# Attention fillers one slot ahead, narrow gate projections as the loaded operand, a position table spread during the values, and scan loads ahead of a wait

## The chip, the cores and the metric

One core of a Trainium2 chip runs the whole program in one launch. The metric is the device time of the execution in microseconds; the kernel before took 3352.78 us, the median of three runs (3352.01 to 3353.17). All arithmetic is float32.

## The reference, cut to what matters

The program is two stacks of layers over 256 tokens of width 2048, one behind the other. The parts that the change touches:

```python
# first block, second layer: attention with three branches and a gate for each of 16 heads x 3
q, g, z = split(h @ w_qg)            # g: 48 columns, z: 3 x 2048 columns
out = sum over branches b of sigmoid(g_b) * attend_b(q, k_b, v_b) * silu(z_b)
x = x + gate * (out @ w_o)           # then the final rmsnorm
# second block: proj = u @ w_in, 11 parts, among them q, k, v and z of a gated delta rule,
q, k, v, beta_logit, a_logit = ...   # beta_logit, a_logit: 8 columns each
for each of 8 heads:                 # chunks of 64 tokens
    T = solve(I + L)                 # triangular, L from k k^T, decay and beta
    scan over 4 chunks with state S
# block attention with a bias by relative distance: rel_bias[bucket(distance), head]
s = q k^T * scale + rel_bias[bucket(i - j), h]
mix = sigmoid(gate_a) * (y_a @ w_gdn) + sigmoid(gate_b) * (y_b @ w_moba)
h = h + mix @ w_out                  # then a gated feed-forward of width 5632
```

## The kernel before, in words

Activations lie transposed: a tensor of 2048 features by 256 tokens is 16 tiles of 128 partitions by 256 columns (`hT`, `xT`). Weights come from HBM in slots of 2 MB, 256 output columns each, through a ring of three (`late_raw`) once the first stages are over; SP issues the loads in program order, and the load of slot n waits until TensorE has finished slot n-3 (`late_load`). Every engine works through one list of instructions in the order written.

A plain slot (`late_plain`) is 32 matmuls, weights as the loaded operand and the activations (256 columns) as the moving one. A split slot (`late_split`, stages in `SPLIT`) saves an eighth of them by sums that VectorE makes of the weights (`dve_sums`, `dve_last_sum`) and of the activations (`dve_half_sums`, once a stage): seven blocks of eight steps, of which the third waits for `late_sums`, the sixth for `late_last`. VectorE joins the parts (`dve_join`). A plain slot is copied out of PSUM by ScalarE (`late_drain`).

Order of the stages on TensorE that matter here: q, gates, zc (8 split slots), attention with the 16 plain slots of zs as fillers, o (output projection), gdn (12 slots), za, qb, kb, vb (4 each), the scan with ga as filler, gb, the second attention with gb2 as filler, the mix (bra, brb), out2, the feed-forward.

The attention works four head groups g, each in six units u (three branches by two token halves: `UNITS`). A unit is: scores on TensorE, mask and maximum on VectorE, exponential on ScalarE, sums and weights on VectorE (`p_ready`), transposes on TensorE, a copy to SBUF by ScalarE (`pT_kept`), values on TensorE (`o_ready`), and VectorE's product with the gate tile `zn` (`o_used`). Between these TensorE runs fillers, counted in matmuls: `FILL0` ahead of a group, and for each unit a number ahead of its transposes and one behind them. In group g they are the zs slots 4g to 4g+3, which hold the gate tiles of the same group; VectorE waits for their drains in units 2 and 4 (`wait_out` in `dve_attend`).

The gates (48 columns) and beta (16 columns) are computed with the activations as the loaded operand: 32 matmuls of 128 tokens each, with 48 or 16 moving columns (`pe_gates`, `pe_beta`).

The delta rule's triangular system is solved on VectorE (`dve_solve`) while TensorE does za, qb, kb, vb. SP moves the system in (`sp_solve`, through `scratch_L`) and the solution out and in again (`sp_solved`, through `scratch_T`), which stands in SP's list between the loads of vb and of ga. ScalarE stages each head of the scan (`act_scan`), then TensorE transposes it.

The position bias: a one-hot table by distance times `rel_bias` (`pe_bias`) gives a row for each head, which goes to HBM (`scratch_R`) and comes back with shifted rows (`sp_bias`). All of it stands behind the first gb slot and the sums of the norms; the mask is added in `dve_qkb`, behind VectorE's norms.

## Time and profile before

| | us or share |
|---|---|
| median of three runs | 3352.78 |
| profiled execution: its own time, span | 3352.57, 3350.8 |
| TensorE busy, weight loads, VectorE, ScalarE | 95%, 87%, 51%, 14% |
| chain that ended last | TensorE 78%, DMA 9%, VectorE 9%, issue 2% |
| attention, its four windows (1137 to 1466) | TensorE busy 303.29 of 329.00, granted clock 0.95 to 0.96 |
| one head group, from scores to scores | 82.2 |
| one split slot (112 records) in the chain of waits | 12.6 |
| a load of 2 MB, issue to landing, median | 8.4 |
| ScalarE's drains of the third and the last vb slot start | 1979.98, 1993.80 |
| granted clock, mean | 0.975 |

How to read it: a row of the timeline is a run of like instructions, with its start and length; the bracket tells how long the engine was idle before, and what ended that. A float32 matmul shows as two records, so x64 are 32 matmuls. The granted clock is a share of 2.4 GHz. Idle time of an engine off the chain costs nothing. TensorE's records overlap a little, so the distance of two starts tells more than a length.

### The profile page before, as it was taken

Reading aid. Unit: us, or ns where it says so; the run is one execution under the profiler, and the core shown is the slowest. Engines: PE = TensorE matmul, PEld = TensorE weight load, DVE = VectorE, ACT = ScalarE, POOL = GpSimd, SP = SyncE. Lnnn points to the kernel's source line nnn. Section 1 sums busy time; section 2 is a strip of 40 time slices with the busy share of each in tenths; the row PEclk is TensorE's granted clock in tenths of the full one; section 3 lists DMA queues with packets and bytes.
Section 4 is the critical chain, followed back from the end, with each engine's and each line's share of the span. In section 5 each row is a group of like instructions: output and inputs, shape, how many; then the busy total and the mean of one; then the engine's idle time right before and its main releaser. Section 6 shows DMA issues by size and latency. Waiting matters only on the chain.

```text
span 3350.8 us, 54055 instructions
## 1 busy us (share of the span) xinstructions
PE 3195.2 (95%) x22956; PEld 2905.7 (87%) x22956; DVE 1721.0 (51%) x2637; ACT 453.2 (14%) x798; POOL 138.0 (4%) x89
## 2 busy tenths in 40 slices
PE   6999998979999999989999999989999999999999
PEld 3777787868889977779888888879999999999999
DVE  5357634453244333346364765566665655555443
ACT  2114410000000122211220002211000000000000
POOL 0003310100000000002000000000010000000000
PEclk8999999989999999999999999999999999999999
DMA  9763457657473322224234442242544444444443
GB/s 409 313 276 127 188 236 320 262 213 289 175 298 150 141 109 107 101 104 173 101 137 179 153 160 101 101 146 97 182 177 154 173 175 157 169 175 157 169 163 138
DMA packets 50952, 599.37 MB, mean 179 GB/s; under 512 B 9511, under 2 KB 12086, under 8 KB 13278
## 3 DMA queue, kind: packets, MB, share of 16 engines
q1 hardware_dynamic: 50782, 596.88, 46.1%
q8 instruction: 134, 2.20, 0.3%
q14 instruction: 36, 0.29, 0.0%
HBM read 593.70 MB, written 3.16 MB: 178 GB/s over the span
## 4 chain that ended last, share of the span: by engine, by line
PE 78%; DMA 9%; DVE 9%; DVEq 2%; issue 2%; SPq 1%; ACT 1%; POOLq 0%; POOL 0%; ACTq 0%
PE bank L2496 24%; PE bank L771 16%; PE bank L720 13%; PE bank L286 9%; DMA ring<-in_t_mod 6%; PE bank L316 3%; DVE E L356 3%; DVE W L2008 2%; PE bank L328 2%; DVE W L2010 1%; PE bank L394 1%; PE aux L1593 1%; PE bank L546 1%; PE aux L1550 1%; PE bank L536 1%
## 5 line engine op out<-in xcount | busy, mean ns | idle before, releaser
L720 PE MATMUL bank<-hT,ring 128*128 128x256 f32 x2496 | 558.4, 383 | 4.3 <-DMA ring<-in_t_ga 4.3
L720 PEld LDWEIGHTS bank<-hT,ring 128*128 128x128 f32 x2496 | 475.9, 192 | 84.6 <-issue 16.8
L2496 PE MATMUL bank<-arena,ring 128*128 128x128 f32 x3440 | 396.4, 275 | 0.0
L2496 PEld LDWEIGHTS bank<-arena,ring 128*128 128x128 f32 x3440 | 390.2, 192 | 0.0
L286 PE MATMUL bank<-arena,ring 128*128 128x256 f32 x1536 | 342.5, 386 | 29.3 <-DMA ring<-in_t_kv 8.9
L286 PEld LDWEIGHTS bank<-arena,ring 128*128 128x128 f32 x1536 | 295.9, 194 | 72.2 <-issue 14.6
L771 PE MATMUL bank<-hT,ring 128*128 128x128 f32 x2624 | 323.0, 278 | 0.0
L771 PEld LDWEIGHTS bank<-hT,ring 128*128 128x128 f32 x2624 | 308.6, 194 | 6.0 <-issue 5.6
L286 PE MATMUL bank<-hT,ring 128*128 128x256 f32 x1024 | 228.0, 385 | 9.2 <-DVE hT L978 4.8
L286 PEld LDWEIGHTS bank<-hT,ring 128*128 128x128 f32 x1024 | 196.8, 193 | 37.8 <-DMA ring<-in_t_q 5.0
L2496 PE MATMUL bank<-hT,ring 128*128 128x128 f32 x1680 | 197.9, 275 | 0.0
L2496 PEld LDWEIGHTS bank<-hT,ring 128*128 128x128 f32 x1680 | 192.7, 192 | 0.1
L356 DVE SCALAR_TENSOR_TENSOR E<-ring,c_act,E 128x512 f32<-128x512 f32 x240 | 182.8, 762 | 18.5 <-issue 0.7
L771 PE MATMUL bank<-arena,ring 128*128 128x128 f32 x1472 | 175.5, 275 | 0.0
L771 PEld LDWEIGHTS bank<-arena,ring 128*128 128x128 f32 x1472 | 170.2, 192 | 0.3
L2587 DVE TENSOR_TENSOR arena<-bank,w_gate 128x256 f32<-128x256 f32 x50 | 21.2, 424 | 204.0 <-ACT rstd L2535 132.5
L2496 PE MATMUL bank<-arena,E 128*128 128x128 f32 x1024 | 119.7, 275 | 0.0
L2496 PEld LDWEIGHTS bank<-arena,E 128*128 128x128 f32 x1024 | 117.0, 192 | 0.0
L316 PE MATMUL bank<-hT,ring 128*128 128x256 f32 x512 | 116.8, 387 | 0.0
L316 PEld LDWEIGHTS bank<-hT,ring 128*128 128x128 f32 x512 | 97.4, 193 | 15.1 <-issue 0.4
L2008 DVE TENSOR_TENSOR W<-E,arena 128x128 f32<-128x128 f32 (+7 forms) x64 | 74.8, 1168 | 44.7 <-issue 27.8
L354 DVE TENSOR_SCALAR E<-ring,c_act 128x512 f32<-128x512 f32 x16 | 8.5, 532 | 168.1 <-DMA ring<-in_t_mod 166.1
(425 smaller groups left out, 3692.2 us busy)
## 6 DMA issues: line engine op xcount, KB each, us to landing
ring<-in_t_mod SPq DMA_DIRECT2D x64, 2048.0 KB, 13.7
ring<-in_t_gu SPq DMA_DIRECT2D x44, 2048.0 KB, 8.2
ring<-in_t_out SPq DMA_DIRECT2D x16, 2048.0 KB, 8.4
ring<-in_t_zs SPq DMA_DIRECT2D x16, 2048.0 KB, 8.4
ring<-in_t_down SPq DMA_DIRECT2D x16, 2048.0 KB, 7.4
ring<-in_t_gdn SPq DMA_DIRECT2D x12, 2048.0 KB, 8.4
ring<-in_t_u SPq DMA_DIRECT2D x8, 2048.0 KB, 8.9
ring<-in_t_z SPq DMA_DIRECT2D x8, 2048.0 KB, 8.6
```

The lines of the kernel that those rows point to most:

```text
L286: last = nc.tensor.matmul(bank[s][:, T * f:T * f + T], w[:, j, P * f:P * f + P], act[:, j, :], start=j == 0, stop=j == kd - 1)
L316: last = nc.tensor.matmul(bank[s][:, T * f:T * f + T], w[:, j, P * f:P * f + P], act[:, j, :], start=j == 0, stop=j == KD - 1)
L328: last = nc.tensor.matmul(bank[s][:, T * f:T * f + T], act[:, j, P * f:P * f + P], w[:, j, :], start=j == 0, stop=j == KD - 1)
L356: nc.vector.scalar_tensor_tensor(a, w, c_act[:, j:j + 1], a, ALU.mult, ALU.add)
L394: last = nc.tensor.matmul(out[32 * q:32 * q + 32, :], c_act[:, j:j + 1].to_broadcast([P, 32]), w[:, j, :], start=a == 0, stop=a == KD // 4 ...
L536: last = nc.tensor.matmul(out[:, T * f:T * f + T], w[:, j, P * f:P * f + P], x[:, j, :], start=j == 0 and f == 0, stop=j == KD - 1 and f == 1)
L546: last = nc.tensor.matmul(out[:, T * f:T * f + T], w[:, j, P * f:P * f + P], x[:, j, :], start=j == 0, stop=j == KD - 1)
L720: last = nc.tensor.matmul(out[:, T * f:T * f + T], w[:, j, P * f:P * f + P], act[:, j, :], start=j == 0, stop=j == kd - 1)
L771: last = nc.tensor.matmul(out[:, P * at:P * at + P], a[:, j, :], tile_at(b, j), start=j == 0 and q in (0, 3), stop=j == half - 1 and q in ...
L1550: last = nc.tensor.matmul(aux[:, nk * h:nk * h + nk], qg[:, h, P * f:P * f + P], keys, start=True, stop=True)
L2008: v.tensor_tensor(tmp, Tsol[:, :, 0:J], row, ALU.mult)
L2496: last = nc.tensor.matmul(out[:, P * q:P * q + P], a[:, j, :], b[:, j, :], start=begins and q == 0 and j == 0, stop=ends and q == len(grou ...
```

## The change

```diff
+def pe_o_first(pe, act, first, count):
+    n = LBASE["o"]
+    w = late_raw[n % LRING][:].rearrange("p (j n) -> p j n", n=SLOT_COLS)
+    out = late_bank(n)[0]
+    old = KD - HPG
+    order = [(f, j) for heads in (range(old), range(old, KD)) for f in range(2) for j in heads]
+    if first == 0:
+        late_ready(pe, n)
+        pe.wait_ge(att_ready, KV - 1)
+    for m in range(first, first + count):
+        f, j = order[m]
+        if m == 2 * old:
+            pe.wait_ge(att_ready, KV)
+        last = nc.tensor.matmul(out[:, T * f:T * f + T], w[:, j, P * f:P * f + P], act[:, j, :],
+                                start=m == 0, stop=m == 2 * KD - 1)
+    if first + count == 2 * KD:
+        last.then_inc(late_done, 1)
...
             late_split(pe, name, s, quarters(act), t_all, (at, at))
+        elif name == "o":
+            pe_o_first(pe, act, O_AHEAD, 2 * KD - O_AHEAD)
...
 gates_ready = sem("gates_ready")
...
+gate_fold, gate_rows = W[:, 1920:1984], W[:, 1664:1920]
+beta_fold, beta_rows = W[:, 1536:1568], W[:, 1280:1536]
...
+    for j in range(KD // 2):
+        for q in range(4):
+            k, first = j + KD // 2 * (q // 2), 16 * (q % 2)
+            last = nc.tensor.matmul(A(3, T, T)[32 * q:32 * q + 32, :], w_gate[:, k, first:first + 32], hT[:, k, :],
+                                    start=j == 0, stop=j == KD // 2 - 1)
+    last.then_inc(gates_summed, 1)
+def pe_gates_fold(pe):
+    pe.wait_ge(folds_ready, 1)
+    pe.wait_ge(gates_raw, 1)
     for f in range(TT):
-        for j in range(KD):
-            last = nc.tensor.matmul(A(3, 48 * f, 48), hT[:, j, P * f:P * f + P], w_gate[:, j, :],
-                                    start=j == 0, stop=j == KD - 1)
+        for at, first, n in ((0, 0, 16), (16, 32, 32)):
+            last = nc.tensor.matmul(A(3, 48 * f + at, n), gate_rows[:, P * f:P * f + P], gate_fold[:, first:first + n],
+                                    start=True, stop=True)
...
+def act_gates_raw(act):
+    act.wait_ge(gates_summed, 1)
+    nc.scalar.copy(gate_rows, A(3, T, T)).then_inc(gates_raw, 1)
...
     for s in range(LCOUNT["zc"]):
+        if s == 1:
+            act_gates(act)
...
 def dve_zc(dve):
+    nc.vector.tensor_tensor(gate_fold, ident[:, 0:64], ident[:, 64:128], ALU.add).then_inc(folds_ready, 1)
...
-FILL0, FILL = 10, [(12, 4), (12, 4), (18, 4), (22, 4), (16, 4), (18, 0)]
-ENDS = {}
-_done = FILL0
-for _u, _pieces in enumerate(FILL):
-    for _place, _count in enumerate(_pieces):
-        for _slot in range(_done // (2 * KD), (_done + _count) // (2 * KD)):
-            ENDS[_slot] = (_u, _place)
-        _done += _count
+FILL0 = 10
+FILLS = [[(12, 4), (12, 4), (18, 4), (22, 4), (14, 4), (18, 2)]] * (KV - 1)
+FILLS += [[(10, 4), (10, 4), (12, 4), (18, 4), (16, 4), (0, 0)]]
+O_FILL = (20, 4)
+O_AHEAD = sum(O_FILL)
+ENDS = []
+for _fill in FILLS:
+    _done, _ends = FILL0, {}
+    for _u, _pieces in enumerate(_fill):
+        for _place, _count in enumerate(_pieces):
+            for _slot in range(_done // (2 * KD), (_done + _count) // (2 * KD)):
+                _ends[_slot] = (_u, _place)
+            _done += _count
+    ENDS.append(_ends)
 def act_attend(act):
+    def gate_slot(s):
+        at = 4 * (s // 4) + HEADS * (1 + s % 4 // 2) + 2 * (s % 2)
+        late_drain(act, "zs", s, zn[:, at:at + 2, :], ACT.Silu)
...
         for k in range(4):
-            if ENDS[k] == (u, place):
-                at = 4 * g + HEADS * (1 + k // 2) + 2 * (k % 2)
-                late_drain(act, "zs", 4 * g + k, zn[:, at:at + 2, :], ACT.Silu)
+            if 4 * g + k + 1 < LCOUNT["zs"] and ENDS[g][k] == (u, place):
+                gate_slot(4 * g + k + 1)
+    gate_slot(0)
...
     pe.wait_ge(kc_kept, 1)
+    late_plain(pe, "zs", 0, hT)
     for g in range(KV):
+        FILL = FILLS[g]
...
                 n = min(count, 2 * KD - first)
-                late_plain(pe, "zs", 4 * g + k, hT, first, n)
+                late_plain(pe, "zs", 4 * g + k + 1, hT, first, n)
...
             done += FILL[u][0]
+            if (g, u) == (KV - 1, ATT - 1):
+                pe_o_first(pe, tiles(B(1)), 0, O_FILL[0])
...
             done += FILL[u][1]
+            if (g, u) == (KV - 1, ATT - 1):
+                pe_o_first(pe, tiles(B(1)), O_FILL[0], O_FILL[1])
...
             v.tensor_tensor(z, z, zn[:, ds(4 * g + HEADS * br, 4), :], ALU.add)
-    dve.drain().then_inc(att_ready, 1)
+        dve.drain().then_inc(att_ready, 1)
...
+def dve_fold_beta(dve):
+    v = nc.vector
+    v.tensor_tensor(beta_fold[:, 0:16], ident[:, 0:16], ident[:, 32:48], ALU.add)
+    v.tensor_tensor(beta_fold[:, 16:32], ident[:, 64:80], ident[:, 112:128], ALU.add)
+    dve.drain()
+    v.tensor_tensor(beta_fold[:, 0:16], beta_fold[:, 0:16], beta_fold[:, 16:32], ALU.add).then_inc(folds_ready, 1)
...
+    flat = w_beta[:].rearrange("p j n -> p (j n)")
+    for j in range(KD // 4):
+        for q in range(4):
+            k = 4 * j + q
+            first = 16 * k - (16 if q == 3 else 0)
+            last = nc.tensor.matmul(A(3, T, T)[32 * q:32 * q + 32, :], flat[:, first:first + 32], hT[:, k, :],
+                                    start=j == 0, stop=j == KD // 4 - 1)
+    last.then_inc(lg_summed, 1)
+def pe_beta_fold(pe):
+    pe.wait_ge(folds_ready, 2)
+    pe.wait_ge(lg_raw, 1)
     for f in range(TT):
-        for j in range(KD):
-            last = nc.tensor.matmul(A(3, 16 * f, 16), hT[:, j, P * f:P * f + P], w_beta[:, j, :],
-                                    start=j == 0, stop=j == KD - 1)
+        last = nc.tensor.matmul(A(3, 16 * f, 16), beta_rows[:, P * f:P * f + P], beta_fold[:, 0:16],
+                                start=True, stop=True)
...
+def act_beta_raw(act):
+    act.wait_ge(lg_summed, 1)
+    nc.scalar.copy(beta_rows, A(3, T, T)).then_inc(lg_raw, 1)
...
     pe.wait_ge(norm_inv, 1 if part == 0 else 2)
-    pe.wait_ge(rel_kept, 1)
...
         dve_sums(dve, "gb", s + 2)
+        if s == 1:
+            dve_bias(dve)
...
 flip, causal_flip = B(2, 3072, P), B(2, 3072 + P, P)
-onehot = B(4, 0, 512)[0:32]
-rel = B(4, 512, 8)[0:32]
-by_dist = B(4, 1024, 512)[0:GH]
+onehot = [st[0][0:32], st[4][0:32]]
+rel = W[0:32, 2000:2008]
+by_dist = [st[6][0:GH], W[0:GH, 1744:2000]]
...
+def sp_rel(sp):
+    sp.wait_ge(head_done, GH + 1)
+    for k in range(2):
+        sp.dma_start(onehot[k], t["onehot"][:, T * k:T * k + T]).then_inc(rel_in, 16)
+    sp.dma_start(rel, t["rel_bias"]).then_inc(rel_in, 16)
+def sp_rel_out(sp):
+    sp.wait_ge(rel_kept, 1)
+    for k in range(2):
+        sp.dma_start(t["scratch_R"][:, T * k:T * k + T], by_dist[k]).then_inc(rel_out, 16)
...
-    sp.wait_ge(oh_kept, GH + 1)
-    sp.dma_start(onehot, t["onehot"]).then_inc(rel_in, 16)
-    sp.dma_start(rel, t["rel_bias"]).then_inc(rel_in, 16)
-    sp.wait_ge(rel_kept, 1)
-    sp.dma_start(t["scratch_R"], by_dist).then_inc(rel_out, 16)
-    sp.wait_ge(rel_out, 16)
+    sp.wait_ge(rel_out, 32)
...
 def pe_bias(pe):
-    pe.wait_ge(rel_in, 32)
-    nc.tensor.matmul(A(3)[0:GH], rel, onehot, start=True, stop=True).then_inc(rel_ready, 1)
+    pe.wait_ge(rel_in, 48)
+    pe.wait_ge(head_done, GH)
+    for k in range(2):
+        last = nc.tensor.matmul(A(3, T * k, T)[0:GH], rel, onehot[k], start=True, stop=True)
+    last.then_inc(rel_ready, 1)
...
     act.wait_ge(rel_ready, 1)
-    nc.scalar.copy(by_dist, A(3)[0:GH]).then_inc(rel_kept, 1)
+    nc.scalar.copy(by_dist[0], A(3, 0, T)[0:GH])
+    nc.scalar.copy(by_dist[1], A(3, T, T)[0:GH]).then_inc(rel_kept, 1)
...
     for s in range(LCOUNT["vb"]):
+        if s == 3:
+            act_bias(act)
...
-def dve_qkb(dve):
+def dve_bias(dve):
...
+def dve_qkb(dve):
...
     sp_solve(sp)
-    for name in ("qb", "kb", "vb"):
+    for name in ("qb", "kb"):
         late_stream(sp, name)
+    sp_rel(sp)
+    late_stream(sp, "vb")
+    late_stream(sp, "ga", 0, 2)
     sp_solved(sp)
-    for name in ("ga", "gb"):
-        late_stream(sp, name)
+    sp_rel_out(sp)
+    late_stream(sp, "ga", 2)
+    late_stream(sp, "gb", 0, 3)
     sp_bias(sp)
+    late_stream(sp, "gb", 3)
...
         late_split(pe, "zc", s, h_quarters, zc_halves, (ZC_H, ZC_H))
+        if s == 0:
+            pe_gates_fold(pe)
     pe_attend(pe)
-    pe.wait_ge(att_ready, 1)
...
         else:
-            late_plain(pe, "gdn", s, hT, ready=(h_ready, 12) if s == AHEAD else None)
+            late_plain(pe, "gdn", s, hT)
+        if s == AHEAD - 1:
+            pe.wait_ge(h_ready, 16)
+            pe_beta(pe)
         if s == AHEAD:
-            pe_beta(pe)
+            pe_beta_fold(pe)
...
         for s in range(LCOUNT[name]):
+            if name == "vb" and s == 3:
+                pe_bias(pe)
             late_plain(pe, name, s, hT, rows=name == "vb")
+    pe.wait_ge(rel_kept, 1)
...
             pe_norm_sums(pe)
-            pe_bias(pe)
...
     drain_to(act, "q", q_all, ACT.Copy, SCALE)
-    act_gates(act)
+    act_gates_raw(act)
...
         act_raw(act, s)
+        if s == AHEAD - 1:
+            act_beta_raw(act)
...
     act_norms(act)
-    act_bias(act)
...
     dve_final0(dve)
+    dve_fold_beta(dve)
```

In words: the zs slot 0 is computed and drained ahead of the first group, and each filler is a matmul of the slot after the one it was; the last group fills with the rest of zs and with 24 of the 32 matmuls of o's slot 0, first those of the heads whose groups are done (`pe_o_first`). The gates and beta load 32 weight columns at a time and move 256 columns of activations, four column groups of the array side by side, each summing its share of the 16 tiles; ScalarE copies the four partial sums, and a matmul with stacked identities (`gate_fold`, `beta_fold`) adds and transposes them. The table product runs ahead of the last vb slot from other buffers, in two halves; its rows go out behind the solver's exchange and come back behind the norms' sums, ahead of the last gb load. The mask is added in VectorE's norms. The first two ga loads stand ahead of SP's wait for the solver.

## Rows read from the trace of the kernel before

**Rows 1.** The waits of TensorE, whole span: us in total, times, longest.

```profile
PE aux L1582 <- DVE arena L1631: 17.9, 4, 4.7
PE aux L2324 <- DVEq L2299: 4.6, 1, 4.6
```

**Rows 2.** Timeline, attention's first group: start, length, engine, line, tile, count, [idle, releaser].

```profile
1169.96 9.66 PE L720 MATMUL bank<-hT,ring 128*128 128x256 f32 x44
...
1174.30 1.23 DVE L1631 TENSOR_TENSOR arena<-arena,small 128x1024 f32<-128x1024 f32 x1
...
1204.98 0.69 DVE L1650 TENSOR_TENSOR arena<-arena,aux 128x512 f32<-128x512 f32 x1 [7.22 <-ACT arena L790]
...
1208.64 1.82 PE L1582 MATMUL aux<-con,arena 128*128 128x128 f32 x8 [4.38 <-DVE arena L1631]
1211.57 3.78 PE L1593 MATMUL aux<-arena,W 128*128 128x512 f32 x4 [1.10 <-ACT arena L1536]
...
1219.72 0.96 PE L1550 MATMUL aux<-W,arena 128*128 128x15 f32 x8
```

**Rows 3.** Windows, TensorE, same group: stretch, us, busy, granted clock, DMA share, GB/s.

```profile
1211.00:1216.00 5.00, 4.43 (x7) 0.53 0.02 7
```

**Rows 4.** Timeline, end of the attention.

```profile
1465.17 15.58 PE L720 MATMUL bank<-arena,ring 128*128 128x256 f32 x64 [3.42 <-DVEq L1656]
...
1467.73 2.52 DVE L861 TENSOR_TENSOR hT<-arena,hT 128x1024 f32<-128x1024 f32 x2
...
1472.87 1.22 DVE L818 TENSOR_TENSOR ring<-ring 128x1024 f32<-128x1024 f32 x1
```

**Rows 5.** Windows, then timeline, around the beta matmuls.

```profile
1616.00:1620.00 4.00, 4.00 (x20) 0.50 0.68 287
...
1611.95 10.87 PE L1765 MATMUL aux<-w_beta,hT 128*128 128x16 f32 x64
...
1622.66 17.02 PE L720 MATMUL bank<-hT,ring 128*128 128x256 f32 x64
```

**Rows 6.** Timeline, gates and the start of zc.

```profile
1022.72 9.12 PE L1470 MATMUL aux<-w_gate,hT 128*128 128x48 f32 x64
...
1025.58 2.52 DVE L861 TENSOR_TENSOR arena<-hT,arena 128x1024 f32<-128x1024 f32 x2
...
1031.64 5.29 PE L771 MATMUL bank<-hT,ring 128*128 128x128 f32 x32
```

**Rows 7.** Timeline, row products of the modulation, in four column groups.

```profile
61.93 3.61 PE L394 MATMUL bank<-ring,c_act 128*32 128x256 f32 x32 [2.42 <-DMA ring<-in_t_mod]
...
247.90 1.93 PE L394 MATMUL bank<-ring,c_act 128*32 128x256 f32 x32
249.76 0.42 PE L1228 MATMUL bank<-arena,E 32*32 32x128 f32 x8
```

**Rows 8.** Chain of waits, scratch_T's landings, then timeline, around the solver's end.

```profile
1787.69 10.28 DMA scratch_L<-E
...
1984.68 2.60 DMA scratch_T<-E
...
DMA to landing us min/median/max: 2.6/3.8/4.7
...
1996.31 0.38 ACT L2044 COPY W<-small 128x2 f32<-128x2 f32 x3
1998.04 6.29 PE L720 MATMUL bank<-hT,ring 128*128 128x256 f32 x14 [4.28 <-DMA ring<-in_t_ga]
```

**Rows 9.** Timeline, norms and position table behind the first gb slot.

```profile
2187.60 6.55 DVE L2220 RECIPROCAL W<-W 128x1024 f32<-128x1024 f32 x1
2188.68 1.87 PE L2279 MATMUL aux<-arena 32*8 32x512 f32 x2 [6.19 <-DMA arena<-in_rel_bias]
...
2196.63 1.22 DVE L825 TENSOR_TENSOR ring<-ring 128x1024 f32<-128x1024 f32 x1 [0.67 <-PE bank L771]
2205.46 1.14 PE L2209 MATMUL aux<-W,ones 1*128 1x512 f32 x8
```

More of the change, by code:

```diff
@@ L1395, in build @@
         gates_ready = sem("gates_ready")
+        gates_summed = sem("gates_summed")
+        gates_raw = sem("gates_raw")
+        folds_ready = sem("folds_ready")
+        gate_fold, gate_rows = W[:, 1920:1984], W[:, 1664:1920]
+        beta_fold, beta_rows = W[:, 1536:1568], W[:, 1280:1536]
         gates_kept = sem("gates_kept")
@@ L1689, in build @@
         qk_ready = sem("qk_ready")
+        lg_summed = sem("lg_summed")
+        lg_raw = sem("lg_raw")
         lg_ready = sem("lg_ready")
```

## The prediction

> **What bounds the kernel now.** I read the waits of TensorE first, since the page shows it busy 95% of the span and the chain of waits is 78% TensorE, then the timeline around each wait, then the granted clock around it. The reader is to see two things. The waits in the changed stretch are few but each costs twice: TensorE stands still, and when it resumes its records are twice as long for some microseconds. In the last unit of a head group, TensorE sits idle 4.38 us, for a softmax weight that VectorE wrote late, then 1.10 us for a copy [rows 2]; the granted clock right behind is 0.53 of 2.4 GHz, close to the 1.2 GHz level [rows 3]. There are four such waits, 17.9 us [rows 1]. Second, matmuls with few moving columns lower the clock without any idle time: after the 64 narrow records of the beta projection the clock is 0.50 [rows 5]. The triangular solver on VectorE fills part of the chain, but it runs beside TensorE's projections and starts when TensorE ends the first za slot (SP's loads wait for it), so it moves with TensorE.
>
> All times below are on the profiled execution (3352.57 us, span 3350.8), which lies 0.2 us under the median of the three runs. The rate at full clock: 44 records of a 256-column projection take 9.50 us from start to start of the next group, 0.216 us a record, and a matmul has two records, so 0.432 us [rows 2].
>
> **Fillers one slot ahead.** Why TensorE waits in unit 5: VectorE's product for unit 4 waited 7.22 us for the ScalarE drain of the fourth gate slot [rows 2], and that slot's matmuls are unit 5's own 18 fillers. Only behind it come the weights, done at 1208.59. One slot ahead, the drain lies in unit 4, and unit 5 should look like unit 3, which has the same shape: there the weights end at 1175.53, 5.6 us behind the start of the fillers (1169.96), while 18 fillers last 7.8 us [rows 2]. So 2.2 us of slack and no wait. Before, from the end of the fillers (1204.26, that is 1208.64 less 4.38) to the next scores at 1219.72 are 15.5 us. After: eight transposes 0.9 (half of 1.82), two fillers 0.86, and the copy still decides, which lets the values start 2.2 us behind the transposes (0.2 to its start, 1.0 for it); values 1.8 at full rate (half of 3.78, less the tail), ten fillers 4.3: 8.2 us. With the 0.86 us of fillers that unit 4 gives up, a group gains 8.1 us, three groups 24.4.
>
> The last group holds 96 gate fillers and 24 matmuls of the output projection's first slot; 116 of them come ahead of unit 5's transposes where 128 did: 5.2 us less; from there to the projection's start the 14.7 us become 7.8 (transposes, four fillers, values, then the same 3.42 us for VectorE's product and two additions [rows 4]), 6.9 more. In front stands the first gate slot, +13.8. So the attention's end comes 24.4 + 5.2 + 6.9 - 13.8 = 22.7 us earlier, and with 24 of the 32 matmuls done. The remaining eight want 3.5 us and about 1.8 more at half rate (the old 64 records took 15.58 instead of 13.8 [rows 4]). They end about when VectorE's half sums are there, 5.1 us behind the start (1470.25 against 1465.17 [rows 4]), and the next slot's first two blocks, 3.6 us, end at 8.9 us, when its weight sums end too (1474.09 [rows 4]). What was 15.4 us becomes 5.3: 10.1 more. **Sum 32.8 us.** I looked for what is late next. ScalarE now drains slot 0 before it stages the first group, beside ten fillers (4.3 us against some 2.9 of copies and drain): covered by 1.4 us. In the last group the drain of the last gate slot stands in front of the exponential of unit 5; 20 fillers (8.6 us) stand over a VectorE chain of about 6.2 us from the end of that unit's subtraction. If each group kept 1 us of wait the sum would be 29; if the half-rate stretch behind the attention went too, 34.5.
>
> **Narrow beta.** Removed: 64 records in 10.7 us, and the slot behind them at 16.9 instead of 13.8, since the clock was 0.50 [rows 5]. Added: 32 records in four column groups, a form the kernel has already: 32 records of a 32-column stationary in 1.93 us [rows 7], 1.86 to the next instruction; and a fold of four narrow records, 0.45. ScalarE's copy (about 0.5) and VectorE's three small additions (0.7) lie beside the slot between. 10.7 + 2.9 (the slot to the next instruction) - 1.86 - 0.45 = **11.3 us**. If the four groups did not overlap, 32 records at 0.216 would be 6.9 instead of 1.9, and 6.4 would be left; nothing else can gain more than 12.
>
> **Narrow gates.** Here the cover is the point. Removed: 64 records in 8.8 us, and 1.5 of the slowed start of the next slot (32 records in 5.29 [rows 6]; at 12.5 us for a split slot's 112 they are 3.6). Added: 64 records at the same form, 3.7 us, and a fold of eight, 0.9. But VectorE's half sums, which this long block hid, end at 1028.10 [rows 6], and the new small addition puts them to 1028.4. TensorE would be ready at 1026.3 and waits 2.1 us. An idle of 2.42 us was followed by 32 records of 3.61 instead of 1.93 us [rows 7], so I price a half-rate stretch at 2 us. Slot 0 began at 1031.5 and ended at 1045.6 (12.5 for a split slot, and the 1.5); now 1028.4 + 12.5 + 2 + 0.9 = 1043.8: **1.8 us**. The gates' sigmoid now stands between ScalarE's first and second zc copies; queued behind it is a copy that VectorE's join wants 5 us into slot 1, and the fold is done at its start, so it costs nothing. Without the clock's fall 3.8; with four groups not overlapping, a loss of 6.
>
> The Trainium skill, TensorEngine Tiling (Array Packing), Key Properties, says that changing the tiling mode drains TensorE; that speaks against both edits. Of the drain the rows show at most 0.2 us, the block of 32 records ending 1.86 us after its start [rows 7]. By that rule, with one matmul's latency of 0.38 us at each of the four changes, an estimate, the forecast would be 1.5 us later.
>
> **Scan loads ahead of the solver's wait.** The solver ends at 1984.68 and its result goes out (2.60 us) and back (up to 4.7) [rows 8], so it is back near 1992. But the scan's first weights are issued behind that: TensorE waits 4.28 us and its first 14 records then take 6.29 instead of 3.0 [rows 8], and the transposes come at 2004.3. ScalarE had staged the head by 1996.69 [rows 8]. Now two slots are loaded. The new cost is the queue: the second is issued when the third value slot ends (about 1979.8), still moving (8.4 us a slot on the page) when the solver's result goes out at 1984.7. The nearest row: the solver's input, issued right behind such a load, landed after 10.28 [rows 8]. From the load's end at 1988.4, half a megabyte takes about 2, so 1990.3, and back at 1995.0. TensorE ends the last value slot at 1994.4 (0.8 later, for the position matmuls, now four records), does the seven fillers to 1997.5, ScalarE stages 2.1 us from 1995.2: transposes at 1997.7. **6.5 us.** Bounds: 7.3 if the exchange isn't delayed, 2 if it waits the full 10.28. SP's issue of the second load is ready 5 us before the solver ends, so the wait does not move. The two new waits on SP, for the heads ahead of the table's loads (with vb's loads queued behind) and for the table's copy ahead of the third ga load, are met some 100 us and some 10 us before they are reached.
>
> **Position table.** Removed: 6.19 us of TensorE's wait, 1.87 for the matmul at half rate, and 2.4 of slow records in the slot behind, which lasts from 2190.55 to 2205.46 where 12.5 would do [rows 9]. But VectorE takes over: its two reciprocals end at 2194.15 [rows 9], whatever TensorE does, and the last-sum of the second gate slot follows a join of 1.8, so it ends near 2197.4 where it ended at 2197.85 [rows 9]. TensorE starts the slot at 2182.5, has five of its seven blocks by 2191.4, and stands for 6.0 us; the two last blocks (3.6 us) then run at half rate, 7.1, to 2204.6 against 2205.5: 0.9 gained out of 10. The other half of the edit is better: the wait of 4.6 us at the second attention [rows 1] ends, since VectorE adds the mask inside its norms, 2.5 us that are covered by a slot of 12.5; with the half-rate stretch behind it (1.5) that is 6.1. **7.0 us**, I take 7.2 with the small shifts. Bounds: 4 if that mask or its transfer (behind nothing now, ahead of one load) is late, 11 if the clock stays up in the stalled slot.
>
> **The sum.** 32.8 + 11.3 + 1.8 + 6.5 + 7.2 = 59.6; 3352.6 - 59.6 = 3293.0 for the execution profiled, and with the 0.2 of the median still **3293 us**. Up to the mix after the second attention nothing but TensorE's queue decides, so the terms add; the feed-forward part is unchanged.
>
> **Rivals.** (1) The solver's exchange is late, chance 0.13. SP has one queue, and the load of 2 MB in front is the change's own. The Trainium skill, DMA: Bandwidth & Descriptors, Queues, rings and completion order, says that descriptors of one ring are consumed in order, so the small transfer cannot overtake. With 10.28 us from 1984.7 it is back at 1999.7, TensorE idles 4.4 us, transposes at 2002: 4.3 us lost, and 2 at half rate: 3299. For it: the row of the solver's input. Against it: that one was issued 0.4 us behind its load, this one about 4.9. (2) Attention keeps a wait in unit 5, chance 0.12: ScalarE's table loads around the moved drains make the exponential late, 2 us a group, and the half rate returns with it (3 us): four times 5 is 20, 3313. For it: each drain between two exponentials brings ScalarE two more table loads. Against it: 2.2 us of slack in unit 3, which has the same chain. (3) The narrow forms do not overlap, 0.04: 5 + 8 lost, 3306. (4) Slower than before, 0.01: with its idle stretches gone, TensorE is granted less in the attention. That must cost over 60 us; the four groups have 303 us of busy TensorE at a mean of 0.96, so it decides below a mean of about 0.8. Against it: the unbroken stretches are at 1.00.
>
> **How the numbers follow.** The forecast has 0.70, its own range 3287 to 3300: the clock in the two stalled places is worth +5 and -2, the bounds of attention +4 and -2. To hold 8 in 10 I reach into rivals 1 and 2: 3286 to 3304. A difference under 0.2% (6.7 us) could not be told from no change. No case but the fourth comes near it: faster 0.98, same 0.01, slower 0.01.
>
> **What would show it.** In the waits, the line of the transposes (L1582) keeps no wait over 0.5 us; if it does, rival 2. A group takes 74 us instead of 82.2. The slot behind the beta matmuls lasts 13.8. The zc stage opens with an idle of 2.1 us behind VectorE's half sums; the second gb slot shows a new idle of about 6 us behind its last-sum, and the second attention none. The transposes of the scan follow the last value slot by about 3.3 us; more than 5 means rival 1. I am wrong in the main if the four attention groups together give less than 28 us.

## The result, and the profile after

The kernel after takes 3292.35 us, the median of four runs (3288.40 to 3293.69); the kernel before, timed beside it, 3352.40 (3350.68 to 3353.17). The ratio is 0.982, interval 0.9805 to 0.9834. The profiled execution took 3291.9 us with a span of 3289.8 and a granted clock of 0.984 (before 0.975). The forecast was 3293.

The changed stretches can be compared to 0.1 us, since each begins and ends with an instruction that both timelines have; the last one alone scatters between executions, by up to 1.7 us (see after_again). All lengths here are from start to start:

| from ... to | before | after | gained | forecast |
|---|---|---|---|---|
| start, first gate matmul | 1022.72 | 1024.54 | -1.8 | 0 |
| first gate matmul, slot 1 of zc | 22.98 | 19.61 | 3.4 | 1.8 |
| slot 1 of zc, slot 1 of o | 434.89 | 402.08 | 32.8 | 32.8 |
| slot 1 of o, the first of the two gdn slots at beta | 117.55 | 117.93 | -0.4 | 0 |
| from there, over both slots and beta, to the 32 records behind them (L1887, L1976 after) | 42.67 | 31.33 | 11.3 | 11.3 |
| these 32 records, the scan's transposes | 363.36 | 357.08 | 6.3 | 6.5 |
| the scan's transposes, the last row of TensorE | 1339.78 | 1330.38 | 9.4 | 7.2 |
| sum | | | 61.0 | 59.6 |

The first line is no part of the change: the stages ahead of the gates are the same code, and over all profiles of this document the first gate matmul starts between 1020.56 and 1025.41 us.

The first view is the waits of TensorE from 1000 to 2300 us, after (us in total, times, longest). To be seen: the 17.9 us of the transposes and the 4.6 of the second attention [rows 1] have no successor. Three waits over 1 us are new, behind VectorE's L847, L1533 and L606; the 3.4 us behind L1718 stood there before [rows 4].

```profile
PE bank L792 <- DVEq L847: 5.8, 1, 5.8
PE bank L524 <- DVEq L1718: 3.4, 1, 3.4
PE bank L792 <- DVEq L1533: 2.0, 1, 2.0
PE bank L792 <- DVEq L606: 1.5, 1, 1.5
...
PE aux L1655 <- ACT arena L1591: 0.7, 3, 0.2
```

The timeline of unit 5 in the first head group, after, answers to [rows 2]. VectorE's product for unit 4 (L1712) waits for nobody, the weights are done at 1213.37, and the fillers end 2.4 us behind them; only the copy leaves TensorE idle, for 0.24 us.

```profile
1207.80 7.93 PE L741 MATMUL bank<-hT,ring 128*128 128x256 f32 x36
...
1209.15 0.68 DVE L1712 TENSOR_TENSOR arena<-arena,aux 128x512 f32<-128x512 f32 x1
...
1212.14 1.23 DVE L1693 TENSOR_TENSOR arena<-arena,small 128x1024 f32<-128x1024 f32 x1
1215.57 1.04 PE L1642 MATMUL aux<-con,arena 128*128 128x128 f32 x8
...
1217.71 1.98 PE L1655 MATMUL aux<-arena,W 128*128 128x512 f32 x4 [0.24 <-ACT arena L1591]
```

The windows view of TensorE over one whole head group, after (us, busy, granted clock, DMA share, GB/s): busy 73.69 of 73.93 us at full clock, where [rows 3] showed 0.53 behind the wait.

```profile
1150.87:1224.80 73.93, 73.69 (x353) 1.00 0.32 122
```

The end of the attention answers to [rows 4]. After the 3.43 us for VectorE's last additions come the remaining eight matmuls of the output projection's first slot, then a wait of 1.53 us for its half sums.

```profile
1440.97 3.72 PE L524 MATMUL bank<-arena,ring 128*128 128x256 f32 x16 [3.43 <-DVEq L1718]
1446.23 3.81 PE L792 MATMUL bank<-arena,ring 128*128 128x128 f32 x32 [1.53 <-DVEq L606]
```

Beta after answers to [rows 5]: 1.86 us to the next start instead of 10.71, the slot behind it at full rate, and the fold of four records.

```profile
1564.16 1.93 PE L1841 MATMUL aux<-hT,w_beta 128*32 128x256 f32 x32
1566.02 14.08 PE L741 MATMUL bank<-hT,ring 128*128 128x256 f32 x64
1579.94 0.51 PE L1850 MATMUL aux<-W 128*128 128x16 f32 x4
```

The gates after answer to [rows 6]: 64 records in 3.66 us, a wait of 1.97 us for the half sums, records at full rate behind it, and a second wait of 0.32 us, for the first slot's weight sums.

```profile
1024.54 3.66 PE L1498 MATMUL aux<-hT,w_gate 128*32 128x256 f32 x64
1030.17 3.81 PE L792 MATMUL bank<-hT,ring 128*128 128x128 f32 x32 [1.97 <-DVEq L1533]
1034.30 5.62 PE L792 MATMUL bank<-arena,ring 128*128 128x128 f32 x48 [0.32 <-DVEq L840]
```

SP's queue after, around the solver's end, answers to [rows 8]: the solver's result goes out at 1939.97, and SP, which waits until it has landed, goes on at 1944.24, after 4.27 us.

```profile
1934.65 0.33 SPq L711 DMA_DIRECT2D ring<-in_t_ga  x1
1939.97 0.33 SPq L2082 DMA_DIRECT2D scratch_T<-E  x1
1944.24 1.35 SPq L2086 DMA_DIRECT2D E<-scratch_T  x2
```

And the stretch of the norms after, timeline, answers to [rows 9]: no table any more, but the second gb slot stands for 5.78 us until VectorE has done both reciprocals, a join and the last sum.

```profile
2132.59 3.35 DVE L2306 RECIPROCAL W<-W 128x512 f32<-128x512 f32 x1 [8.17 <-ACT W L2278]
2136.06 6.55 DVE L2308 RECIPROCAL W<-W 128x1024 f32<-128x1024 f32 x1
2144.55 1.22 DVE L846 TENSOR_TENSOR ring<-ring 128x1024 f32<-128x1024 f32 x1
2145.86 3.64 PE L792 MATMUL bank<-hT,ring 128*128 128x128 f32 x16 [5.78 <-DVEq L847]
2149.33 1.95 PE L792 MATMUL bank<-E,ring 128*128 128x128 f32 x16
```

### The profile page after: what moved, and what is told of

It is laid out like the page before. It is cut to its first block, busy times and chain, and to the rows that moved or that the text cites. A ratio compares the mean times of both kernels' runs of the same rounds, so it can differ in the third digit from the quotient of the medians.

```text
span 3289.8 us, 54033 instructions
## 1 busy us (share of the span) xinstructions
PE 3160.6 (96%) x22938; PEld 2877.1 (87%) x22938; DVE 1723.0 (52%) x2641; ACT 453.8 (14%) x801; POOL 139.8 (4%) x89
## 4 chain that ended last, share of the span: by engine, by line
PE 84%; DMA 8%; DVE 5%; DVEq 1%; issue 1%; ACT 0%; SPq 0%; POOLq 0%; POOL 0%; ACTq 0%
PE bank L2600 24%; PE bank L741 18%; PE bank L792 16%; PE bank L286 10%; DMA ring<-in_t_mod 7%; PE bank L316 3%; DVE E L356 3%; PE bank L738 2%; PE bank L328 2%; PE bank L394 1%; PE bank L567 1%; PE aux L1608 1%; PE bank L557 1%; PE aux L1655 1%; DMA ring<-in_t_kv 1%
## 5 line engine op out<-in xcount | busy, mean ns | idle before, releaser
L286 PEld LDWEIGHTS bank<-arena,ring 128*128 128x128 f32 x1536 | 296.8, 194 | 73.1 <-issue 14.7
```

Of the source, the lines that this page charges most:

```text
L286: last = nc.tensor.matmul(bank[s][:, T * f:T * f + T], w[:, j, P * f:P * f + P], act[:, j, :], start=j == 0, stop=j == kd - 1)
```

## The experiments

All were made from the kernel after. The times of one kernel scatter by some 3 us between executions, so each verdict rests on the length of its own stretch in one profile. no_o, long_idle and one_group were run once, so their times have no interval.

**after_again.** The kernel after, run again with the second set of experiments: 3291.01 us, ratio 0.9819 (0.9805 to 0.9832).

> The kernel after, unchanged, as the base for the runs beside it. Expected 3290 to 3293. Profiles so far put the first gate matmul anywhere from 1021.1 to 1024.5 us (the stages ahead of it are unchanged and wait for weights from HBM); theory: all of the scatter between executions is made there, so from the first gate matmul to the end this one takes 2258.4 us again, within 0.5. Rival: later stages scatter too, by more than 1 us.

From the first gate matmul to the last row 2258.48 us, in the first profile 2258.41. The stages after the gates repeat here. The rival is partly true too: in the experiments that leave it as it is, the stretch behind the scan's transposes took up to 1.7 us more than in the kernel after. The timelines show where. The difference lies in the second gb slot, in the 32 records behind the wait for VectorE: start to start they took 5.28 to 6.70 us in ten profiles, and 5.35 to 6.50 where the wait was the same 5.78 us. In one_group, whose edits are far ahead of it:

```profile
2152.97 3.78 PE L792 MATMUL bank<-hT,ring 128*128 128x128 f32 x16 [5.78 <-DVEq L847]
2156.55 2.99 PE L792 MATMUL bank<-E,ring 128*128 128x128 f32 x16
```

In the kernel after the second of these rows is 1.95 us. So the same wait gives a slow stretch of differing length, and a comparison across it is uncertain by over 1 us.

**back_fill.** The old `act_attend` and `pe_attend`, and no matmuls of the output projection inside the last unit, with

```diff
-FILLS = [[(12, 4), (12, 4), (18, 4), (22, 4), (14, 4), (18, 2)]] * (KV - 1) ...
+FILL0, FILL = 10, [(12, 4), (12, 4), (18, 4), (22, 4), (16, 4), (18, 0)]
```

> The kernel after with the attention's fillers alone as before (gate slots beside the group that uses them, no matmuls of the output projection inside). Theory, fillers: the wait of the transposes returns four times, about 4.4 us each, with a granted clock near 0.53 behind it, a head group takes 82.2 instead of 73.9 us, and the kernel 32.9 more: 3325. Rival, the group is shorter because of other edits (clock, transfers): then less than 20 of the 33 come back and the group stays under 80 us.

3323.47 us, ratio 0.992 (0.9903 to 0.9936). To slot 1 of o 32.7 us more. Its waits at the transposes and the values are those of before to the digit, and behind them the clock is near half again (waits, then windows):

```profile
PE aux L1625 <- DVE arena L1674: 17.9, 4, 4.7
PE aux L1636 <- ACT arena L1579: 4.4, 4, 1.1
```

```profile
1208.20:1212.00 3.80, 3.72 (x5) 0.50 0.02 4
```

The placing of the fillers, gate slots and output projection together, makes the whole of that term. The rival falls.

**no_o.** Which part of it is the output projection's 24 matmuls inside the last unit?

```diff
-O_FILL = (20, 4)
+O_FILL = (0, 0)
```

> The kernel after without matmuls of the output projection inside the last attention unit: all 32 come behind it. Theory, as the prediction books them (10.1 of the last group's gain with the 5.2 of half sums hidden): the last unit's weights, which the 20 matmuls cover (8.6 us), are waited for, about 5 us, and the copy behind them 1.1; in exchange the half sums' wait of 1.5 goes, since 14 us of matmuls stand over them. 5 to 8 slower. Rival: the matmuls only change places and nothing was hidden by them: within 1.5 us.

5.6 us more to slot 1 of o (3296.51 us in one run). The timeline shows the two waits back and the half sums' wait gone:

```profile
1428.64 1.97 PE L1644 MATMUL aux<-con,arena 128*128 128x128 f32 x8 [5.46 <-DVE arena L1695]
1431.71 3.78 PE L1657 MATMUL aux<-arena,W 128*128 128x512 f32 x4 [1.10 <-ACT arena L1593]
1435.28 15.26 PE L526 MATMUL bank<-arena,ring 128*128 128x256 f32 x64
1450.38 3.73 PE L794 MATMUL bank<-arena,ring 128*128 128x128 f32 x32
```

The matmuls are worth 5.6 us as cover; by difference the other 27 come from the order of the gate slots, which was not undone alone.

**back_beta.** The 32 matmuls with 16 moving columns again, behind the next slot as before, and no fold.

```diff
+last = nc.tensor.matmul(..., hT[:, j, P * f:P * f + P], w_beta[:, j, :], ...)
```

> The kernel after with the beta projection alone as before: activations loaded, 16 moving columns, 64 records. Theory: 64 records in about 10.7 us and the slot behind them at about 16.9 instead of 13.9 us, with a granted clock near 0.50: 11.3 more, 3303.5. Rival, the clock falls only with the longer history of idle stretches that the kernel before had: then the slot behind stays at 14 and only 8.4 come back.

3299.99 us, ratio 0.9849 (0.9832 to 0.9865). 9.7 us more in its stretch, where 11.3 were expected (timeline, then windows):

```profile
1577.46 9.39 PE L1837 MATMUL aux<-w_beta,hT 128*128 128x16 f32 x64
1586.69 16.87 PE L741 MATMUL bank<-hT,ring 128*128 128x256 f32 x64
```

```profile
1577.50:1580.50 3.00, 3.00 (x29) 1.00 0.65 175
1580.50:1583.50 3.00, 3.00 (x24) 0.77 0.99 426
1583.50:1586.60 3.10, 3.10 (x16) 0.50 0.24 100
```

The slot behind is slow again (16.87 us), without the idle stretches that the attention had before, so these matmuls are enough to bring the clock down; the rival falls. But the 64 records took 9.23 us to the next start and in the kernel before 10.71: there the clock was at 0.50 already 4 us into the block [rows 5], here it was at 0.77 in the second three microseconds. What made it fall some 1.5 us sooner there stays open, and with it 1.5 of the 11.3 us.

**back_gates.** The same for the 48 gate columns: activations loaded again, no fold, and the sigmoid at its old place.

> The kernel after with the gate projection alone as before: activations loaded, 48 moving columns, 64 records. Two readings of the gain. As predicted (1.8 gained: the stall on the half sums costs 2.1 and the clock after it 2): this kernel is 1.8 slower. As the profile after reads (stall 1.97, clock 1.00 behind it, 3.3 gained): from the first gate record to slot 1 of zc 22.9 instead of 19.6 us, 3.3 slower, 3295.6, and a granted clock below 1 again in the slot behind the 64 records.

From the first gate matmul to slot 1 of zc it took 22.99 us against 19.61: 3.4 more, as the profile read and not as predicted. The median, 3292.95 (ratio 0.9829, 0.9813 to 0.9846), cannot tell 1.8 from 3.4. The 64 records and the 32 behind them, which drop to half rate again:

```profile
1021.95 9.15 PE L1496 MATMUL aux<-w_gate,hT 128*128 128x48 f32 x64
1030.91 5.26 PE L792 MATMUL bank<-hT,ring 128*128 128x128 f32 x32
```

**long_idle.** Needless subtractions ahead of the half sums.

```diff
+for _ in range(2):
+    dve_half_sums(dve, h_quarters, zc_halves, (0,))
 dve_half_sums(dve, h_quarters, zc_halves)
```

> The kernel after with two needless VectorE subtractions (about 2.8 us with their drains) ahead of the half sums, so that TensorE idles 4.8 instead of 1.97 us behind the gate matmuls. It prices the term that was wrong. Theory: an idle of 2 us leaves the granted clock at 1, one over 4 us does not; then slot 1 of zc starts 2.8 + 2 later, with the clock near 0.5 behind the idle. Rival: behind a block of narrow weights the clock does not fall at all (few columns loaded, little to throttle): 2.8 later and the clock 1.00.

3296.00 us in one run. The idle became 4.58 us, and slot 1 came 3.7 later, where 4.8 were expected (2.6 of idle, 1.6 of slow records, less some 0.5 for the later wait of 0.32 that it hides and for overlap). Timeline, then windows:

```profile
1031.83 5.44 PE L792 MATMUL bank<-hT,ring 128*128 128x128 f32 x32 [4.58 <-DVEq L1535]
```

```profile
1031.80:1034.80 3.00, 2.97 (x15) 0.56 0.00 0
```

In the kernel after, the same view shows for the records behind 1.97 us of idle, and behind 3.43 at the end of the attention:

```profile
1030.20:1034.00 3.80, 3.78 (x32) 1.00 0.01 2
...
1440.90:1444.70 3.80, 3.72 (x16) 1.00 0.00 0
```

So the price of a fall was about right (1.6 against my 2); wrong was that it falls at 1.97 us. The rival falls: the clock does drop behind narrow weights, after a longer idle. The length of the idle alone does not decide, though. The kernel before had the same wait at the end of the attention, 3.42 us [rows 4], but 4.38 and 1.10 us of idle shortly ahead of it (the last group repeats [rows 2]), and the clock behind it was at half:

```profile
1465.17:1467.17 2.00, 2.00 (x5) 0.50 0.00 0
```

**one_group.** Loops of both narrow blocks exchanged.

```diff
-for j in range(KD // 2):
-    for q in range(4):
+for q in range(4):
+    for j in range(KD // 2):
```

> The kernel after with the loops of both narrow blocks exchanged: the matmuls of one column group follow each other (16 or 8 of them) instead of alternating over the four groups; same work. Theory: the four groups overlap only when matmuls of different groups stand next to each other. Then 64 gate records take 13.8 us instead of 3.7 and the 32 beta records 6.9 instead of 1.9, and the half sums are there when TensorE comes: 8 + 5 = 13 more. Rival: a narrow loaded operand is cheap by itself, with 0.058 us a record in either order: no change.

```profile
1023.77 11.50 PE L1498 MATMUL aux<-hT,w_gate 128*32 128x256 f32 x64
...
1568.62 4.59 PE L1841 MATMUL aux<-hT,w_beta 128*32 128x256 f32 x32
```

The same matmuls take 11.50 instead of 3.66 us, and 4.59 instead of 1.93; 5.2 and 2.7 more in the two stretches, 7.9 together where 13 were expected (3300.15 us in one run). The groups overlap when neighbours in the list belong to different groups; the rival falls. My 13.8 and 6.9 were both 2.3 too long. Both blocks have three changes of group in this order, so the difference may be the overlap at these changes; that was not tested. The Trainium skill, TensorEngine Tiling (Array Packing), Key Properties, says that different tiles can load weights and multiply in parallel; the trace agrees for neighbours, and shows that the order decides.

**back_scan.** The first two ga loads behind the solver's wait again.

```diff
-late_stream(sp, "ga", 0, 2)
 sp_solved(sp)
-late_stream(sp, "ga", 2)
+late_stream(sp, "ga")
```

> The kernel after with the loads of the first two ga slots again behind the wait for the solver. Theory: TensorE waits about 4.3 us for the first ga load and its records are then slow: the scan's transposes come 6.3 to 7.3 us later, 3299. Rival, the transposes wait for the solver's exchange or ScalarE's staging in any case: under 3 us. Also read: the solver's result, out and in, lands after 2.6 us behind no load and took 4.27 behind one; if the queue is the cause, it is 2.6 again here.

5.7 us more to the transposes, where 6.3 to 7.3 were expected; 3293.57 us, ratio 0.983 (0.9814 to 0.9846). Timeline (for the wait of 3.91 us the view names no releaser; the load of the slot, issued at 1940.76, was what stood there before [rows 8]):

```profile
1935.80 0.33 SPq L2082 DMA_DIRECT2D scratch_T<-E  x1
1938.44 1.35 SPq L2086 DMA_DIRECT2D E<-scratch_T  x2
...
1950.04 4.95 PE L741 MATMUL bank<-hT,ring 128*128 128x256 f32 x14 [3.91 <-issue]
```

The 14 records behind the wait took 4.95 us, in the kernel before 6.29 [rows 8], so less came back. SP goes on 2.64 us behind the exchange's start when no load stands ahead, 4.27 with one: the load in front costs the exchange 1.6 us. The Trainium skill, DMA: Bandwidth & Descriptors, Queues, rings and completion order, has descriptors of a ring consumed in order; this pair of rows agrees, but it cannot tell that order from two transfers that share the bandwidth.

**back_mask** (`dve_bias` at the head of `dve_qkb` again) and **back_table** (product, copies and transfers of the table back behind the sums of the norms).

> The kernel after with the two mask additions alone back behind VectorE's norms and the join of the last gate slot; table and transfers stay as after. Theory: the second attention waits 4.6 us again and half rate follows, 6.4 slower. Rival: that wait was made by the late transfer of the table, which is 40 us earlier now: then the attention waits under 3 us (2.4 us of additions, nothing else).

> The kernel after with the table's product and transfers alone back behind the sums of the norms; the mask additions stay in the norms. Theory: TensorE waits about 6.2 us for the table, but the 5.8 us behind VectorE's last sum vanish in exchange, so only 2.7 us are lost (0.9 by the prediction), as long as the biases land before VectorE adds them. Rival: the biases, read back behind the last gb load, land after VectorE asks for them and the norms stall: 5 us or more lost.

back_mask: 7.5 us more in its stretch, where 6.4 were expected; 3297.85 us, ratio 0.9839 (0.9824 to 0.9854). The wait at the second attention is back:

```profile
PE aux L2427 <- DVEq L2399: 4.6, 1, 4.6
```

Of the 7.5 us, some 4.7 are the wait and 2.7 the slow records behind it.

back_table: 2.1 more than in the kernel after, 3291.37 us, ratio 0.9824 (0.9809 to 0.9839). The same stretch differs by 1.7 between profiles that have the same code there, so against these it costs only 0.4 at the least, and the medians (3291.01 for the kernel after beside it) cannot tell it from nothing. TensorE waits 6.28 us for the table, and the wait behind L847 is gone:

```profile
2133.33 1.87 PE L2370 MATMUL aux<-arena 32*8 32x512 f32 x2 [6.28 <-DMA arena<-in_rel_bias]
2135.13 5.41 PE L792 MATMUL bank<-hT,ring 128*128 128x128 f32 x32
```

Both theories hold. The mask was the larger part, although it is two additions of 1.22 us. The ten microseconds of TensorE's waits and slow records around the table were worth 2.1 at most, since VectorE's reciprocals stand behind them.

**recips.** Can that wait be taken away?

```diff
-v.reciprocal(norm_rows[:, 0:512], ...)
-v.reciprocal(norm_rows[:, 512:1536], ...)
+v.reciprocal(norm_rows[:, 512:1024], ...)
 for s in range(2):
     dve_join(dve, "gb", s, two_tiles(gb_all, s))
     dve_last_sum(dve, "gb", s + 1)
+    if s == 0:
+        v.reciprocal(norm_rows[:, 1024:1536], ...)
     dve_sums(dve, "gb", s + 2)
+    if s == 0:
+        v.reciprocal(norm_rows[:, 0:512], ...)
```

TensorE takes the parts in the order 1, 2, 0.

> The kernel after with the order of VectorE's work at the norms changed: the first 512 columns of reciprocals, then the join of gate slot 0 and the last sum of slot 1, then the other two thirds of the reciprocals around the next slot's sums. Theory: the 5.78 us for which TensorE stands still in the second gb slot exist because 9.9 us of reciprocals stand ahead of that last sum; the idle and 1.7 us of records at half rate behind it go, 7.4 faster than the kernel after. Rival: VectorE is short of time in that stretch whatever the order, and the wait moves to the third or the fourth gb slot: under 3 us faster.

3284.36 us, ratio 0.98 (0.9787 to 0.9814), 6.65 under the kernel after beside it; 5.8 in its stretch against the kernel after, where 7.4 were expected (up to 7.5 against the other profiles with that slot's code). The cause is shown: the 5.78 us are gone from the second slot. 1.55 came back in the third, with the records behind at full rate:

```profile
2153.34 2.05 PE L792 MATMUL bank<-hT,ring 128*128 128x128 f32 x16 [1.55 <-DVEq L847]
```

**best.** The last third of the reciprocals under `if s == 1`, and the half sums for zc earlier:

```diff
+            if before_bias:
+                before_bias(dve)
             dve_mod_bias(dve, name)
...
-            dve_mods(dve, "q")
+            dve_mods(dve, "q", dve_zc_halves)
```

Here `dve_zc_halves` is the head of `dve_zc`: the sum for `gate_fold` and the half sums.

> Two orders of VectorE changed in the kernel after. (1) recips, and the last third of the reciprocals now behind the last sum of the third gb slot, which was 1.55 us late there: 7.4 us faster than after by the stretch of the norms, where recips gave 5.9. (2) The activations' half sums for zc stand ahead of VectorE's wait for the last sums of the modulation, beside the last q slot, where VectorE has been idle for 25 us: the waits of 1.97 and 0.32 behind the gate matmuls go, 2.3. Together 9.7 faster than after: 3281.3. Rival: the next wait takes over (the weight sums of the first zc slot, or the fourth gb slot): under 7.

3279.70 us (3278.41 to 3281.43), ratio 0.9782 (0.9769 to 0.9796). 2.6 us are gained in the gates (17.01 instead of 19.61), 7.6 in the norms, 10.2 together against the kernel after (9.7 expected); no wait is left in either:

```profile
1022.88 3.66 PE L1500 MATMUL aux<-hT,w_gate 128*32 128x256 f32 x64
1026.47 3.84 PE L794 MATMUL bank<-hT,ring 128*128 128x128 f32 x32
```

## Why the prediction was right, and where it was not

**Bounds and attention.** Right, in sum and in the mechanism: "only the copy decides" is the 0.24 us, a group takes 73.9 us (74 forecast), and undoing the placing alone gives 32.7. One piece was wrong without a price. I had the eight matmuls at half rate behind the 3.4 us of waiting; they ran at full clock and ended early. But the half sums, forecast at 5.1 us behind the start, came at 5.26, so TensorE stood 1.53 us and the stretch is what was forecast, 5.3: VectorE sets it, whatever TensorE's clock. That the error cost nothing is luck. (The 14.7 us of the last group are 14.5 in the trace before.)

**Beta.** 11.3 and 11.3; the overlap of the four groups, the fold and the fall of the clock are each shown. Undone alone it gave 9.7; some 1.5 of the 11.3 hang on how early the clock fell in the kernel before. The 1.5 us that the prediction estimated for drains at changes of tiling do not show: the beta block's 32 records end 1.86 us after their start here too.

**Gates.** The step that failed is "so I price a half-rate stretch at 2 us", taken from one row with an idle of 2.42 [rows 7]. The wait was forecast to 0.1 us (1.97 for 2.1), but the clock stayed at 1.00. The prediction had the other end ("without the clock's fall 3.8"); measured are 3.4, and 0.3 of the rest is the second wait, for the weight sums, which it had not seen.

**Scan.** 6.3 against 6.5. The exchange out took 4.27 us, not the 5.6 of the sum, and its return, issued at 1944.2 and 1944.9, landed after 3.9 to 4.6 us: 1949.5 at the latest. ScalarE ended the last vb drain at 1950.2 and staged the head behind it, and for that TensorE's weight load waited 0.36 us. So the first rival did not come about, with 0.7 us to spare. The position matmuls cost 1.0, not 0.8.

**Position table and mask.** The step was mis-sized by 2.2: 9.4 for 7.2. The stall was as forecast (5.78 for 6.0), but "the two last blocks then run at half rate, 7.1" held for one: 16 records near half rate took 3.47, the other 16 ran at full rate, 5.35 together. In other profiles the same two blocks took up to 6.70, so up to 1.3 of these 1.75 us is scatter of the slow stretch. The table gave 2.65 instead of 0.9. The mask gave 6.75 instead of 6.1, since the slow records behind the old wait cost 2.0 and not 1.5. Undone alone, mask and table cost 7.5 and 0.4 to 2.1.

**Rivals.** The second (a wait kept in unit 5) shows in no row: the longest wait there is 0.24. The third did not come about, because the list alternates the groups; in the other order it comes in part. The fourth: the attention ran at 1.00.

**The time.** The stretches behind the first gate matmul gave 62.8 us against 59.6, and the start was 1.8 later in this execution. That the total is only 0.7 us off is luck: the 3.2 us gained beyond the forecast and the later start nearly cancel.

## What to carry to other kernels

A wait of the busiest engine for a second engine can be a wait for its own later work: follow it back over two releasers, and if the chain returns to matmuls of the same unit, move these one slot ahead. When a stall is taken away, work out what the second engine does in that same stretch, whatever the first one waits for: ten microseconds gone gave 2.7 at most, and another order of VectorE's instructions gave 6 more. If an engine stands idle ahead of a wait (VectorE 25 us here), work that is late behind the wait and doesn't depend on it can go there. And compare the same stretch in several profiles before pricing it: behind the same wait one took 1.2 us more than another.

## What the runs showed of the hardware

TensorE idle for 1.53, 1.97 and once 3.43 us kept a granted clock of 1.00; idle for 4.4 to 5.8 us it came back at 0.50 to 0.56. Where idle stretches follow each other it came back slow after less: at 0.50 after 3.42 us in the kernel before, and at twice the record length after 2.42 in the first stages [rows 7]. How long it stays slow varies behind the same idle: the 32 records behind 5.78 us took 5.35 to 6.50 us. A price for the slow stretch needs the length of the idle and what lay before it, and has a spread of its own.

The 64 records with 16 moving columns brought the granted clock to 0.50 with TensorE busy all the while.

Moving activations of 256 columns with 32 loaded columns in four column groups cost 0.06 us a record if the groups alternate, 0.14 to 0.18 if they don't (3.66 and 1.93 us against 11.50 and 4.59 in one_group).

A reciprocal of 512 columns takes VectorE 3.35 us, an addition of 1024 columns 1.22: per column 5.5 times as much. The Trainium skill, VectorE: DVE Perf Modes, Walkthrough: the 8-slice pipeline in each mode, calls it an iterative divide with a repeat count of 8; the rows show that it is dear, not the count.
